# Output projection of a gated decoder step: weights stationary and channel-major, or merged rows stationary and token-major

## What is computed

```
def merge(gate_logits, b_gate, outs, w_branch, w_out):
    ...
    return jnp.sum(gates * proj, axis=-2) @ w_out
...
x = x + merge(gl, b_gate[l], (out_a, out_b, out_c), w_branch[l], w_out[l])
...
y_prompt = rmsnorm(xp, g_final)
y_sample = rmsnorm(xs, g_final)
```

## Time and profile before

| | us |
|---|---|
| median of 3 runs | 914.23 |
| lowest, highest | 912.98, 914.28 |
| profiled execution: span from first to last instruction | 911.0 |
| profiled execution: own device time | not given |
| TensorE busy in the span | 870.7 (96%) |
| VectorE, ScalarE, GpSimd busy | 415.1, 394.9, 95.8 |

### The profile page before, as it was taken

One profiled execution on the slowest core, in us unless ns is written; L12 is line 12 of the kernel. 1 busy time (PEld: TensorE's weight loads), 2 busy tenths in 40 slices (PEclk: granted clock), 3 DMA queues, 4 the chain that ended last, 5 costly groups with the idle time before them and its releaser, 6 DMA issues.

```text
span 911.0 us, 16721 instructions
## 1 busy us (share of the span) xinstructions
PE 870.7 (96%) x7062; PEld 843.4 (93%) x7062; DVE 415.1 (46%) x700; ACT 394.9 (43%) x659; POOL 95.8 (11%) x136
## 2 busy tenths in 40 slices
PE   4999999999999999999999999999999999999991
PEld 4899999999999999999999999999899999999990
DVE  4663213223344346643325888654344454445333
ACT  4752222327566766332232256332234563433334
POOL 4100000000000101300001247001020000000000
PEclk9999999999999999999999999999999999999996
DMA  9764222141132434962446971426561432252102
GB/s 259 224 192 140 93 92 76 63 137 50 59 127 81 151 95 153 356 207 94 164 139 210 318 236 47 163 71 229 187 227 56 136 103 83 102 188 87 64 2 94
DMA packets 86147, 126.53 MB, mean 139 GB/s; under 512 B 3201, under 2 KB 72833, under 8 KB 86081
## 3 DMA queue, kind: packets, MB, share of 16 engines
q1 hardware_dynamic: 71808, 75.50, 26.1%
q0 software_dynamic: 13984, 49.02, 15.4%
q10 hardware_dynamic: 288, 1.05, 0.3%
HBM read 113.37 MB, written 12.19 MB: 138 GB/s over the span
## 4 chain that ended last, share of the span: by engine, by line
PE 92%; DMA 2%; ACT 2%; DVE 1%; issue 1%; DVEq 0%; POOL 0%; SPq 0%; ACTq 0%
PE mm L848 79%; DMA raw<-in_w_mem_kv_dram 2%; PE p L859 1%; PE p L826 1%; PE p L828 1%; PE p L827 1%; PE p L1009 1%; PE p L1039 1%; PE p L983 1%; PE p L980 1%; PE p L956 1%; PE p L1087 1%; PE p L979 1%; PE p L997 0%; ACT mz L509 0%
## 5 line engine op out<-in xcount | busy, mean ns | idle before, releaser
L848 PE MATMUL mm<-h_lo,w_hi 128*128 128x260 f32 x1536 | 315.5, 287 | 0.0
L848 PE MATMUL mm<-h_hi,w_hi 128*128 128x260 f32 x1536 | 309.1, 283 | 0.0
L848 PE MATMUL mm<-h_hi,w_lo 128*128 128x260 f32 x1536 | 308.4, 282 | 0.0
L848 PEld LDWEIGHTS mm<-h_lo,w_hi 128*128 128x128 f32 x1536 | 237.0, 188 | 9.5 <-issue 8.0
L848 PEld LDWEIGHTS mm<-h_hi,w_lo 128*128 128x128 f32 x1536 | 236.4, 188 | 0.0
L848 PEld LDWEIGHTS mm<-h_hi,w_hi 128*128 128x128 f32 x1536 | 236.4, 188 | 0.0
L1128 DVE TENSOR_TENSOR w_lo<-raw,w_hi 128x1024 fp32r<-128x1024 f32 x136 | 165.6, 1219 | 108.0 <-ACT w_hi L504 104.0
L504 ACT ACTIVATE w_hi<-raw 128x1024 fp32r<-128x1024 f32 x136 | 143.3, 1054 | 14.0 <-DMA raw<-in_w_in_dram 6.7
L848 PE MATMUL mm<-x_lo,w_hi 128*128 128x260 f32 (+1 forms) x512 | 115.7, 287 | 1.4 <-DVE w_lo L1128 1.4
L848 PE MATMUL mm<-x_hi,w_hi 128*128 128x260 f32 (+1 forms) x512 | 113.8, 283 | 0.0
L848 PE MATMUL mm<-x_hi,w_lo 128*128 128x260 f32 (+1 forms) x512 | 113.7, 283 | 0.0
(11 more groups left out here) (289 smaller groups left out, 829.3 us busy)
## 6 DMA issues: line engine op xcount, KB each, us to landing
raw<-in_w_in_dram SPq DMA_DIRECT2D x44, 1024.0 KB, 5.3
raw<-in_w_branch_dram SPq DMA_DIRECT2D x12, 1024.0 KB, 5.0
raw<-in_w_mem_kv_dram SPq DMA_DIRECT2D x8, 1024.0 KB, 6.5
gate<-in_cache_mem_k_dram POOLq DMA_DIRECT2D x16, 512.0 KB, 6.4
tok<-in_cache_mem_v_dram POOLq DMA_DIRECT2D x14, 512.0 KB, 4.6
tok<-in_state_gla_dram POOLq DMA_DIRECT2D x8, 512.0 KB, 6.1
out_dram<-tok POOLq DMA_DIRECT2D x8, 512.0 KB, 7.5
work<-scr_q POOLq DMA_DIRECT2D x8, 512.0 KB, 5.3
```

The costliest lines, as they stand in the source:

```text
L848: ins = MM(mm[:, j % 2, a, 0:c1 - c0], wp[:, j, k, :], xp[:, k, c0:c1], start=(k == 0 and wp is w_hi and xp is xl), stop=(k == KT - 1 and ...
```

## The change

The output projection leaves the scheme of the blocks. It becomes token-major: for 128 tokens the merged rows `h_lo`/`h_hi` are the stationary operand and the split weights move, so that the result has tokens on its partitions and the transposes go.

- The split weights of output channels 0 to 511 lie in `w_hi`/`w_lo`, those of 512 to 1023 in `x_hi`/`x_lo`, which are free after PC (`out_hi`, `out_lo`).
- A ring (`out_ring`) is one accumulation of 24 matmuls: 8 input tiles, 3 products. Rings run over 4 token tiles with channels 0 to 255, then 4 with 256 to 511 (256 moving columns, two blocks of 128 from neighbouring slots of `w_hi`), each in a PSUM bank of its own. After the sample come 4 rings with channels 512 to 1023 (512 columns), one for each token tile.
- The 8 sample rows no longer ride along. Their high and low parts are copied side by side into `sums`, 40 columns, and 2 x 16 matmuls of 512 columns give both products at once on PSUM rows 0 to 7 and 32 to 39 (`out_sample`).
- The first 512 channels of every token tile are squared and multiplied by g_final early (`out_first`, `out_scale`). After the wide ring of a token tile, that tile is finished alone: addition (`out_add`), square, square root, reciprocal, scaling of its lower half by ScalarE and of its upper by VectorE (`out_rest`, `out_last`), and its store over SyncE's queue, for the last tile in two halves.

```diff
-            for n in range(2):
-                sp.wait_ge(sem("y_ready"), n + 1)
+            for n in range(NT - 1):
+                sp.wait_ge(sem("y_low"), n + 2)
+                sp.wait_ge(sem("y_high"), n + 2)
                 sp.dma_start(y_prompt[0, n * P:(n + 1) * P, :], tok[:, n, :]).then_inc(sem("y_stored_sp"), 16)
+            n = NT - 1
+            sp.wait_ge(sem("y_low"), NT + 1)
+            sp.dma_start(y_prompt[0, n * P:(n + 1) * P, 0:512], tok[:, n, 0:512]).then_inc(sem("y_stored_sp"), 16)
+            sp.wait_ge(sem("y_high"), NT + 1)
+            sp.dma_start(y_prompt[0, n * P:(n + 1) * P, 512:D], tok[:, n, 512:D]).then_inc(sem("y_stored_sp"), 16)
...
+            def out_rest(rows, col, scaled):
+                r = rows.shape[0]
+                act.wait_ge(sem("o_sq"), NT + 1)
+                link(A(o_junk[0:r, :], rows[:, 512:D], ACT.Square, accum_out=osq[0:r, col, 1:2]))
+                act.wait_ge(sem("o_bias"), NT + 1)
+                A(rstd[0:r, col:col + 1], osq[0:r, col, 1:2], ACT.Sqrt, scale=1.0 / D, bias=obias[0:r, col, :]).then_inc(sem("y_rt"), 1)
+                act.wait_ge(sem("o_scaled"), NT + 1)
+                act.wait_ge(sem("y_rs"), scaled)
+                A(rows[:, 0:512], rows[:, 0:512], ACT.Copy, scale=o_inv[0:r, col:col + 1]).then_inc(sem("y_low"), 1)
...
+            def out_ring(rows, hi, lo, n, bank, tiles, gate_k):
+
+                ts = slice(n * P, (n + 1) * P)
+                for k in range(KT):
+                    if gate_k:
+                        pe.wait_ge(sem("m_lo"), k + 1)
+                    for xp, wp in ((h_lo, hi), (h_hi, lo), (h_hi, hi)):
+                        ins = MM(bank[:, 0:tiles], xp[:, k, ts], rows(wp, k), start=(k == 0 and xp is h_lo),
+                                 stop=(k == KT - 1 and xp is h_hi and wp is hi))
+                ins.then_inc(sem("o_prod"), 1)
...
+            def out_project():
+                for q in range(2):
+
+                    pe.wait_ge(split_done, first("OUT") + 2 * q + 2)
+                    for n in range(NT):
+                        if q == 0 and n % 2 == 0:
+                            pe.wait_ge(evac_done, first("OUT") - 1 + n // 2)
+                        out_ring(lambda w, k: w[:, 2 * q:2 * q + 2, k, :], w_hi, w_lo, n, o_bank[4 * q + n], 256, q == 0 and n == 0)
+                pe.wait_ge(sem("o_sample"), 2)
+                pe.wait_ge(sem("o_zeros"), 1)
+                pe.wait_ge(sem("o_added"), 1)
+                out_sample(lambda w, k: w[:, :, k, :], w_hi, w_lo, o_bank[0])
+                pe.wait_ge(split_done, first("OUT") + KT)
+                pe.wait_ge(sem("o_added"), 2)
+                out_sample(lambda w, k: w[:, k, 0:512], x_hi, x_lo, o_bank[1])
+                for n in range(NT):
+                    pe.wait_ge(sem("o_added"), n + 3)
+                    out_ring(lambda w, k: w[:, k, 0:512], x_hi, x_lo, n, o_bank[n + 2], 512, False)
...
+            def out_stage():
+                V.memset(sums[:, :, B:32].bitcast(F32), 0.0).then_inc(sem("o_zeros"), 1)
+                out_add(0)
+                out_add(1)
+                out_lo(6)
+                out_lo(7)
...
+                for n in range(NT):
+                    out_add(2 * NT + n)
+                    out_last(tok[:, n, :], n, n + 2)
```

More of the change, by code:

```diff
@@ L64 @@
 XN = 5
[L67 removed]
+TR = {n: KT * i for i, n in enumerate(["K", "V", "BV", "AV"])}
 ST = {n: KT * i for i, n in enumerate(["PB", "AU", "PA", "PC"])}
[L70 removed]
+IRREGULAR = {"K", "V", "BZ", "CQ", "GB", "AZ", "PB", "AV", "AU", "GA", "PA", "CZ", "GC"}
 def first(name):
@@ L257, in bass_gated_parallel_step @@
         p67 = ctx.enter_context(nc.psum_tensor("p67", [P, 2, 512], F32))
+        o_bank = [mm[:, n // 2, n % 2, :] for n in range(4)] + [p45[:, 0, :], p45[:, 1, :], p67[:, 0, :], p67[:, 1, :]]
         p45_8 = p45[:, :, :].rearrange("p a (b c) -> p (a b) c", c=P)
@@ L1068, in att_pv, with out_sample @@
                 ins.then_inc(sem("apv_done"), 1)
+            def out_ring(rows, hi, lo, n, bank, tiles, gate_k):
[7 more added lines that the diff above has]
+                ins.then_inc(sem("o_prod"), 1)
+            def out_sample(rows, hi, lo, bank):
+                for k in range(KT):
+                    for wp in (lo, hi):
+                        ins = MM(bank[0:40, :], sums[:, k, :], rows(wp, k), start=(k == 0 and wp is lo),
+                                 stop=(k == KT - 1 and wp is hi))
+                ins.then_inc(sem("o_prod"), 1)
+            def out_project():
[12 more added lines that the diff above has]
+                out_sample(lambda w, k: w[:, k, 0:512], x_hi, x_lo, o_bank[1])
+                for n in range(NT):
+                    pe.wait_ge(sem("o_added"), n + 3)
+                    out_ring(lambda w, k: w[:, k, 0:512], x_hi, x_lo, n, o_bank[n + 2], 512, False)
             pe.wait_ge(sem("ident_ready"), 1)
@@ L1077, in _ @@
                 ins.then_inc(sem("memT_done"), 1)
-            for name in NAMES:
+            for name in NAMES[:-1]:
                 if name == "QK":
@@ new lines, in out_last @@
+            def out_last(rows, col, scaled):
+                r = rows.shape[0]
+                dve.wait_ge(sem("y_rt"), scaled)
+                V.reciprocal(o_inv[0:r, col:col + 1], rstd[0:r, col:col + 1]).then_inc(sem("y_rs"), 1)
+                dve.wait_ge(sem("y_rs"), scaled)
+                V.scalar_tensor_tensor(out=rows[:, 512:D], in0=rows[:, 512:D], scalar=o_inv[0:r, col:col + 1], in1=gf_bc[0:r, 512:D],
+                                       op0=ALU.mult, op1=ALU.mult).then_inc(sem("y_high"), 1)
```

141 lines of the change are left out of this document (83 added, 58 removed).

## The result

The changed kernel takes **908.69 us** (median of four runs, 907.39 to 908.96), the kernel before 914.25 (four runs, 912.98 to 914.41): a ratio of 0.9946, 95% interval 0.9934 to 0.9959, so 3.7 to 6.0 us less; the two medians alone lie 5.6 us apart. The forecast was 908.0 us in a range of 905.8 to 910.9, faster. The profiled execution of after took 908.95 us with a span of 907.1.

What follows compares the result with a forecast made beforehand. TensorE's streaming and the tail after its last product were taken as the bound: +2.1 us streaming, +1.7 waiting, -10.0 tail, together -6.2 on the 911.0 span; 904.8 + 3.2 gave 908.0 us, range 905.8 to 910.9.

Steps and rivals of the forecast that it cites:

- The narrow rings: Output projection, 8 rings of 24 matmuls with 256 moving columns: 0.1185 us a matmul, 22.8 us together.
- The rival of the moving operand in pieces: 256-column rings and sample: each moving block costs a 128-column matmul, 0.216 us a matmul, 930 us in all; chance 4%.
- The new wait: Ring 0 of the output projection: TensorE waits at 842.0 for channel tile 7's low part, 1.7 us added.
- the prediction's own sign of being wrong: End of the output projection: the working is wrong if TensorE ends later than 894.5.
- The wide matmuls and the sample: Output projection, 128 matmuls of 512 columns: 0.2268 us each, 29.0 us together, 7.3 us of that for the sample.
- The rival by which 512 columns would cost what 256 do: Wide matmuls: weight load sets the pace, 512 columns start every 0.120 us, 13.7 us less, 894; chance 1%.
- The middle: Output projection between first ring and tail: weight splits, sample's root with table load and early stores, costed at nothing.
- The tail: After TensorE's last result: last tile's addition, square, root, scaling, two stores and end of span, 11.6 us in place of 21.6.
- The rule that was weighed against it: Last store: some 2 us fixed per transfer plus bytes over 436 GB/s, landing 2.96 us after scaling, time 908.8.
- The step from the span to the time: End of the sum: 3.2 us between span and median kept, so 904.8 + 3.2 = 908.0.
- The clock: Rival at the 842 wait: granted clock falls to 0.50, 49 us more if for good; chance 1%.
- the main step: End of the kernel: a tail of 11.6 us (893.2 to 904.8) in place of 21.6, -10.0 us.

Runs made afterwards that it cites:

- e1: Changed kernel with the first two narrow rings interleaved, each input tile feeding two token tiles before the next is wanted; 906.37 us, ratio 0.9923 to the kernel before.
- e6: Changed kernel with the last token tile stored by one DMA of 512 KB in place of two of 256 KB; 907.29 us, ratio 0.9941 to the kernel before.
- e3: Changed kernel with no token tile stored before the last one is scaled; 911.14 us, ratio 0.9984 to the kernel before.
- e4: Changed kernel with squares, roots, scalings and stores of all token tiles held until after the last addition; 913.18 us, ratio 1.0002 to the kernel before.
- e2: Changed kernel with the sample's two products run over one input tile of eight, output incomplete; 901.26 us, ratio 0.9868 to the kernel before.

## Why the prediction was right, and where it wasn't

**The narrow rings.** 0.1185 us a step was forecast, 0.1184 to 0.1185 measured. The rival of the moving operand in pieces falls: neither two nor four blocks show.

**The new wait.** Forecast 1.7 us at 842.0 for the last `h_lo`; it was 1.74 and 0.10 for the resuming stream, at 843.7 in an execution that was 1.7 us late already. That lateness also puts TensorE's last matmul at 895.1, beyond the prediction's own sign of being wrong (later than 894.5); less the 1.72 it is 893.4, against the 892.6 to 893.3 of the forecast. The sign had been set without room for what happens upstream. e1 shows that it cost its full size.

**The wide matmuls and the sample.** 0.2268 was taken from the attention, where the rows give 2.50 / 11 = 0.2273 in both kernels. In the output projection they came 0.2302 apart, and the sample's 0.2316. Over 128 matmuls that is 0.5 us, the larger part of the 0.6 by which the last result was later after the start of the projection than forecast (54.3 us against 53.7). Why the same shape has a slightly longer step here is not settled. The rival by which 512 columns would cost what 256 do fell clearly; the 131 ns that the Trainium skill (TensorE: Matmul & The Clock Gate, "Back-to-back issue gap") gives for them in a sustained stream was 230 ns here.

**The middle.** Nothing of it reached the path, as costed. Low parts 6 and 7 were ready at 856.75, 2.3 us later than forecast, 1.7 of it from upstream, and TensorE wanted the first of the second half of the weights at 869.5. The table load came at 876.3, beside the first wide ring, as forecast. Since the sample's part lies ahead of the wide rings, its products cost their full stream but its normalization nothing.

**The tail.** 2.72 us were forecast from the last result to the last scaling, and 2.79 measured; term by term the addition was 0.69 for 0.67, the square 0.63 for 0.62, the scalings 0.75 and 0.72 for 0.69. The stores then moved as forecast: 0.83 us to the first byte and 1.3 us of bytes were costed, and after has 0.87 (898.33 to 899.2) and 1.4. What the working had wrong is the landing. It put the landing at the last byte, 2.15 us behind the scaling, and it came 0.4 us behind that byte, 2.7 us behind the scaling. From the landing to the end were to be 6.7 us and it was 6.1. The two errors cancel, since both hang on the same point: from the last byte to the end were to be 6.7 us and it was 6.5, in after and in e6. By issue and landing the rows show 2.0 and 2.3 us for 256 KB and 2.6 for 512 KB (e6). The rule that was weighed against it is a part of some 2 us that doesn't depend on size, plus the bytes (the Trainium skill, DMA: Bandwidth & Descriptors, "Anatomy of one DMA"). That section speaks of transfers issued by GpSimd, which the prediction did not say, and these stores are SyncE's. Its 2.96 was nearer to 2.7 than the row-based 2.15, but it is too large by 0.3 to 0.6 us for each store (for 256 KB it gives 2.6, for 512 KB 3.2). The 6.7 us were a choice between 6.35, counted from the landing of the sample's store, and 7.1, counted from the end of the bulk. After, e3, e4 and e6 all have 6.1 us from the last landing to the end. The whole tail was forecast at 11.6 us and is 11.58.

**The step from the span to the time is where the working failed, and its number came out by luck.** "The median of the runs, 914.23, is 3.2 us above the span, and I leave these 3.2 as they are." The time of an execution is 1.7 to 1.9 us above its own span in every run of this study (908.95 and 907.1 in after). The 3.2 mixed a span of the lower group with a median of the upper. It amounts to taking 6.2 us off the median of before, and that fits because three of four runs fell into the upper group in both kernels; beside four runs like those of e6, all in the lower group with a median of 907.29, the same 908.0 would have been too high. The right working would have been: span 904.8 and 1.8 around it, 906.6 in the lower group (measured 907.1 to 907.4) and 908.1 in the upper (908.4 to 909.0). What is left, a gain of 5.6 and not 6.2 us, is the later last result above. In the profile, the span came 2.3 us above the forecast 904.8, 1.7 of it from upstream.

**The range.** Its lower end of 906.2 does not follow from its terms: 908.0 less 0.35, 0.5 and 0.7 is 906.45, and an overlap of them would leave less to take off. Nothing hangs on it, since the range was then widened to 905.8.

**The clock.** The rival did not come true, but the evidence against it was thin. "TensorE was idle for 1.1 of the 4 us from 67 with the clock at 1.00 throughout" was one execution; in others the clock falls behind this very wait, so that 1% for the new wait said more than one trace could. The price of 49 us was for a clock that stays down; the fall at 69 us cost 1.5, since the clock came back while TensorE went on streaming. At the new stand it didn't fall in any of the six traces that have it (after, e2 to e6). In the windows of after that follow the stand:

```profile
842.00:846.00 4.00, 2.43 (x20) 2.22 (x20) 2.56 (x4) 2.18 (x4) 0.00 (x0) 1.00 0.78 262
846.00:866.00 20.00, 20.00 (x170) 19.92 (x169) 10.61 (x18) 6.85 (x13) 0.53 (x1) 1.00 0.17 55
```

**The stores in the tail.** e3 and e4 bear out the larger part of the main step, the tail of 11.6 for 21.6 us: put back, the stores alone cost 3.95 us and the whole finishing 5.9, with the saving of 5.6 gone. The remaining 4.1 of the 10.0 are only in part taken apart.

## What to carry to other kernels

A product whose rows are what the next step reduces over can be finished row tile by row tile, and then only one tile's chain and store lie behind the last matmul; exchanging the operands for that is worth while even if it costs some streaming, but only if each tile is in fact finished in its own ring (e4 has the exchange without that, and gains nothing). Look at what the exchanged order wants first: it may want all the input tiles within half the time, as ring 0 does, and interleaving two outputs over the same inputs takes that wait away. And compare a profiled execution with its own time before comparing it with a median, since the two may belong to different groups.

## What the runs showed of the hardware

- TensorE's granted clock fell behind a wait of 1.27 us at 68 us in six of ten traces (0.52 to 0.70 in the 3 us from 69, against 1.00 in the other four), for a cost of some 1.5 us; behind a wait of 1.57 us at 844 it fell in none of six traces.
- 32 matmuls of 512 moving columns with 40 stationary columns cost 0.232 us each, as much as with 128: few stationary columns save nothing.
- The same shape, 512 columns in fp32r with its weight load, started every 0.227 us in the attention and every 0.230 in the output projection of the same trace.
- Two stores of 256 KB issued by SyncE behind one another landed in 2.0 and 2.3 us, one of 512 KB alone in 2.6; in both cases the bytes took 1.4 us (364 and 375 GB/s), from some 0.8 us behind the first issue to 0.4 us before the last landing. From the last landing to the end of the span 6.1 us passed in after, e3, e4 and e6, whatever had been stored.
